# Forget-gate attention: projections by head half, heads placed between k steps, one PSUM bank per head

## The reference

```python
def forgetting_mixer(h, w_in, b_f, w_out):
    proj = h @ w_in                                   # 1024 -> 3 * 1024 + 16
    qkv = proj[..., :3 * ATTN_WIDTH].reshape(B, S, 3, N_HEADS, HEAD_DIM)   # 16 heads of 64
    q, k, v = qkv[:, :, 0], qkv[:, :, 1], qkv[:, :, 2]
    log_f = log_sigmoid(proj[..., 3 * ATTN_WIDTH:] + b_f)
    c = cumsum(log_f, axis=1)
    # per head:  s = q k^T / 8 + c_i - c_j, causal;  p = softmax(s);  o = p v
    return o @ w_out
```

## Time and profile before

| what | value |
|---|---|
| time, median of 3 runs | 2292.36 us (2290.62 to 2293.33) |
| span of the profiled execution, first to last instruction | 2288.1 us |
| PE busy | 2171.5 us, 95% of the span |
| DVE busy / ACT busy | 1228.2 us (54%) / 1006.8 us (44%) |
| mean granted TensorE clock | 0.940 of full |
| the fox stage, first q0 matmul to first FFN matmul | 1950.58 to 2089.11 us |

### The profile page before, as it was taken

One profiled execution on the slowest core, in us unless ns is written; L12 is line 12 of the kernel. 1 busy time (PEld: TensorE's weight loads), 2 busy tenths in 40 slices (PEclk: granted clock), 3 DMA queues, 4 the chain that ended last, 5 costly groups with the idle time before them and its releaser, 6 DMA issues.

```text
span 2288.1 us, 27158 instructions
## 1 busy us (share of the span) xinstructions
PE 2171.5 (95%) x9922; PEld 1783.3 (78%) x9930; DVE 1228.2 (54%) x1280; ACT 1006.8 (44%) x1233; POOL 262.7 (11%) x387
## 2 busy tenths in 40 slices
PE   7999979899999999889999899999999999999997
PEld 5887857788878878677788787778777887887886
DVE  4555589755555556698654544235325545545554
ACT  5445744544444446645444344224314444454442
POOL 1000195000000000680000023002100000000000
PEclk9999989999999999989999999579758999999999
DMA  6554433445545554325455545015203554424552
GB/s 233 197 183 176 167 142 123 165 174 189 195 150 202 190 196 166 138 98 185 164 184 189 186 147 184 1 60 185 87 0 127 186 190 177 147 93 147 184 183 100
DMA packets 53476, 354.22 MB, mean 155 GB/s; under 512 B 7440, under 2 KB 8080, under 8 KB 11536
## 3 DMA queue, kind: packets, MB, share of 16 engines
q1 hardware_dynamic: 53392, 353.10, 43.2%
HBM read 352.03 MB, written 1.05 MB: 154 GB/s over the span
## 4 chain that ended last, share of the span: by engine, by line
PE 82%; DVE 8%; ACT 3%; issue 2%; DVEq 2%; POOL 1%; POOLq 1%; ACTq 0%; DMA 0%; SPq 0%
PE psum L1460 55%; PE psum L1516 15%; PE psum L1606 4%; PE psum L1635 3%; DVE wlo L849 3%; DVE arena L1023 2%; PE psum L1616 2%; DVEq L1017 1%; ACT whi L478 1%; PE psum L1526 1%; PE psum L1558 1%; PE psum L1604 1%; PE psum L1472 1%; DVE arena L1034 0%; ACT arena L608 0%
## 5 line engine op out<-in xcount | busy, mean ns | idle before, releaser
L849 DVE TENSOR_TENSOR wlo<-raw,whi 128x2048 fp32r<-128x2048 f32 x325 | 745.6, 2296 | 531.4 <-ACT whi L478 531.4
L1460 PE MATMUL psum<-whi,xTh 128*128 128x512 f32 (+1 forms) x1968 | 781.4, 397 | 32.5 <-DVE xTl L856 17.1
L1460 PE MATMUL psum<-whi,xTl 128*128 128x512 f32 (+1 forms) x1968 | 768.1, 390 | 0.0
L1460 PE MATMUL psum<-wlo,xTh 128*128 128x512 f32 (+1 forms) x1968 | 767.0, 390 | 0.0
L478 ACT ACTIVATE whi<-raw 128x2048 fp32r<-128x2048 f32 x325 | 620.8, 1916 | 280.9 <-PE psum L1516 151.0
L1460 PEld LDWEIGHTS psum<-whi,xTh 128*128 128x128 f32 x1968 | 375.0, 191 | 111.2 <-DVE xTl L856 17.2
L1460 PEld LDWEIGHTS psum<-whi,xTl 128*128 128x128 f32 x1968 | 374.2, 190 | 78.4
L1460 PEld LDWEIGHTS psum<-wlo,xTh 128*128 128x128 f32 x1968 | 375.3, 191 | 72.8
L1516 PE MATMUL psum<-whi,braT 128*128 128x512 f32 x1056 | 337.4, 390 | 6.6 <-DVE braT L967 6.6
L1516 PEld LDWEIGHTS psum<-whi,braT 128*128 128x128 f32 x1056 | 198.2, 188 | 48.9 <-issue 5.4
L1516 PE MATMUL psum<-wlo,braT 128*128 128x512 f32 x528 | 205.5, 389 | 0.0
(11 more groups left out here) (187 smaller groups left out, 1572.0 us busy)
## 6 DMA issues: line engine op xcount, KB each, us to landing
raw<-w_stream SPq DMA_DIRECT2D x327, 1024.0 KB, 4.8
bias<-chunks SPq DMA_DIRECT2D x18, 256.0 KB, 5.0
x<-x_in SPq DMA_DIRECT2D x1, 1024.0 KB, 5.0
arena<-gate_w SPq DMA_DIRECT2D x2, 512.0 KB, 4.8
arena<-fins SPq DMA_DIRECT2D x2, 512.0 KB, 5.6
out<-x SPq DMA_DIRECT2D x1, 1024.0 KB, 4.0
con<-consts SPq DMA_DIRECT2D x1, 784.0 KB, 11.9
vec<-vecs SPq DMA_DIRECT2D x2, 94.5 KB, 4.0
```

Source lines behind the costliest of these rows:

```text
L849: TT(wlo[:, r], raw[:, r], whi[:, r].bitcast(F32), ALU.subtract).then_inc(lo_done, 1)
L1460: ins = pe.matmul(dst(rb), s(kt)[:, rows], w[:, r, at_:at_ + cols], start=start and n == 0 and k == 0, stop=stop and n == len(kts) - 1 and ...
```

## The change

Only the fox stage changes; the arithmetic is the same.

1. The order of units becomes f, q0, k0, v0, q1, k1, v1, and the weight stream is laid out to match. `sums` moves from behind q0 to behind the first k step of q0.
2. `whole` and `attention` are no longer called here. PE gets an order of single k steps (`step`), with the pieces of the heads between them: `scores_of`, `turn_p`, `pv`, and the turns of single row groups (`heads_turn`). Heads 0 to 7 lie between the k steps of q1, k1 and v1.
3. Heads 8 to 15 lie between the k steps of the output projection. Its k steps alternate between the two column halves (`out(0, kt)`, `out(1, kt)`), in an order in which each needs only output tiles that are there; the output's split tiles lie in `braT` and `latT`, and there are six turns of them instead of four (`FOX_O_TILES`).
4. A head has one PSUM bank (4 + h%2) for scores, turned probabilities and output in succession; scores of head h wait until DVE has taken the output of head h-2 out (`fox_out`).
5. DVE takes over the copy of the turned probabilities from ACT (`turned_out`) and scales each head's output by itself (`o_out`, 16 times a reciprocal, a drain and one operation).
6. At the end of the stage the norm's transposes stand between the last k step of column half 0 and that of half 1.

```diff
-FOX_TURNS = (NORM_TURNS + [(f"{qk}{n}", "act" if n % 2 == 0 else "dve") for qk in "qk" for n in range(8)]
-             + [(f"o{n}", "split") for n in range(4)])
+FOX_TURNS = (NORM_TURNS + [(f"{qk}{n}", "act" if n % 2 == 0 else "dve") for half in range(2) for qk in "qk" for n in range(4 * half, 4 * half + 4)]
+             + [("o1", "split")] + [(f"o{n}", "split") for n in range(2, 6)])
+FOX_TURNS.insert([n for n, _ in FOX_TURNS].index("k4"), ("o0", "split"))
+FOX_O_TILES = [(0, 1), (2, 3), (4,), (5,), (6,), (7,)]
...
 ACT, new order from the splits on
+                split(b, 7)
+                exp(0)
+                exp(1)
+                split(b, 8)
+                rows("q", 1)
+                split(b, 9)
+                exp(2)
...
+                exp(14)
+                exp(15)
+                o_hi(4)
+                o_hi(5)
+                split(b, 16)
                 next_norm(b)
...
 DVE
+                def turned_out(h):
+                    dve.wait_ge(p_turned, fox_place(b, h))
+                    if h >= 2:
+                        dve.wait_ge(pv_done, fox_place(b, h - 2))
+                    dve.tensor_copy(x_pt[h % 2], psum[:, 4 + h % 2, 0:3 * P]).then_inc(pt_dve, 1)
+                def o_out(h):
+                    dve.wait_ge(exp_done, fox_place(b, h))
+                    dve.reciprocal(rden[:, 2 * h:2 * h + 2], den[:, 2 * h:2 * h + 2])
+                    dve.drain()
+                    dve.wait_ge(pv_done, fox_place(b, h))
+                    TT(x_o[:, :, h * HD:(h + 1) * HD], psum[:, 4 + h % 2, 0:2 * HD]...).then_inc(fox_out, 1)
...
+                upto(6)
+                v_out(0)
+                upto(7)
+                largest(0)
+                largest(1)
+                upto(8)
+                turned_out(0)
+                o_out(0)
+                turned_out(1)
+                upto(9)
+                largest(2)
+                o_out(1)
...
+                residual(units.place("wo0"), 1.0, ready, ((0, 0), (0, 1)))
+                next_norm(b)
+                residual(units.place("wo0"), 1.0, ready, ((1, 0), (1, 1)))
+                upto(16)
...
 PE
-                todo = [None, turns("q", x_q, 0), turns("q", x_q, 1), turns("k", x_k, 0), turns("k", x_k, 1), first_scores]
-                for n, name in enumerate(("q0", "q1", "k0", "k1", "v0", "v1")):
-                    whole(b, units, name, 1 + 2 * n, 2, W, xh, xl, never, between=todo[n])
-                    if n == 0:
-                        sums()
-                turns_left(b, plan, "k7")
-                run(first=2)
-                pe.wait_ge(o_done, o_count[0])
-                row_turns(b, plan, ("o0", "o1"), x_o)
-                out_proj(b, plan, units, "o", 13, lambda: row_turns(b, plan, ("o2", "o3"), x_o[:, :, W:]))
+                step("q0", 1, 0)
+                sums()
+                for kt in range(1, 8):
+                    step("q0", 1, kt)
+                for kt in range(8):
+                    step("k0", 3, kt)
+                    if kt >= 4:
+                        heads_turn("q", kt - 4)
+                for kt in range(8):
+                    step("v0", 5, kt)
+                    if kt % 2:
+                        heads_turn("k", kt // 2)
+                step("q1", 7, 0)
+                scores_of(0)
+                step("q1", 7, 1)
+                step("q1", 7, 2)
+                scores_of(1)
+                step("q1", 7, 3)
+                step("q1", 7, 4)
+                turn_p(0)
+                step("q1", 7, 5)
+                step("q1", 7, 6)
+                pv(0)
+                turn_p(1)
+                step("q1", 7, 7)
...
+                out(0, 5)
+                scores_of(14)
+                pv(13)
+                out(1, 5)
+                turn_p(14)
+                scores_of(15)
+                o_turns(4)
+                pv(14)
+                out(0, 6)
+                turn_p(15)
+                out(1, 6)
+                pv(15)
+                o_turns(5)
+                out(0, 7)
+                norm_turns(b.next)
+                out(1, 7)
```

More of the change, by code:

```diff
@@ L806, in fox @@
[L806 to L828, removed]
+                split(b, 1)
+                split(b, 2)
+                rows("q", 0)
+                act.wait_ge(fox_pe, 1)
+                c = psum[:, 4, 0:RB * NH].rearrange("p (r h) -> p r h", r=RB)
+                act.activation(x_q[:, :, :, HD + 1], c, ACT.Copy)
@@ new lines, in fox @@
+                split(b, 9)
+                exp(2)
+                tiles_out("q", 4)
+                exp(3)
+                split(b, 10)
+                tiles_out("q", 6)
+                exp(4)
+                exp(5)
+                rows("k", 1)
+                split(b, 11)
+                o_hi(0)
+                tiles_out("k", 4)
+                exp(6)
+                split(b, 12)
+                exp(7)
+                tiles_out("k", 6)
+                split(b, 13)
+                exp(8)
@@ L1277, in v_out, with largest @@
                     ins.then_inc(udve, 1)
-                upto(10)
-                v_out(0)
-                upto(12)
[L1282 to L1285, removed]
+                def largest(h):
+                    dve.wait_ge(s_in, fox_place(b, h))
+                    for rb in range(RB):
+                        ins = dve.reduce_max(negmax[:, 2 * h + rb:2 * h + rb + 1], psum[:, 4 + h % 2, rb * P:rb * P + (rb + 1) * P], AX, negate=True)
+                    ins.then_inc(max_done, 2)
@@ new lines, in fox @@
+                turned_out(3)
+                largest(4)
+                o_out(3)
+                turned_out(4)
+                largest(5)
+                tiles_out("q", 7)
+                upto(11)
+                o_out(4)
+                turned_out(5)
+                o_lo(0)
+                largest(6)
+                o_out(5)
+                tiles_out("k", 5)
+                upto(12)
+                turned_out(6)
+                largest(7)
+                o_out(6)
+                turned_out(7)
@@ new lines, in fox @@
+                tiles_out("k", 7)
+                o_out(7)
+                v_out(1)
+                largest(8)
+                upto(13)
+                o_lo(1)
+                largest(9)
+                turned_out(8)
+                o_out(8)
+                turned_out(9)
+                largest(10)
+                o_out(9)
+                turned_out(10)
+                largest(11)
+                o_out(10)
+                turned_out(11)
+                upto(14)
+                o_lo(2)
@@ new lines, in fox, with ready @@
+                largest(12)
+                o_out(11)
+                turned_out(12)
+                largest(13)
+                upto(15)
+                o_lo(3)
+                o_out(12)
+                turned_out(13)
+                largest(14)
+                o_out(13)
+                turned_out(14)
+                largest(15)
+                o_lo(4)
+                o_out(14)
+                turned_out(15)
+                o_out(15)
+                o_lo(5)
+                def ready(c, rb):
+                    dve.wait_ge(slot_used, b.slot + 16 + c)
@@ new lines, in scores_of @@
+                def scores_of(h):
+                    if h % 2 == 0:
+                        if h // 2 % 2:
+                            pe.wait_ge(tdve, b.tdve + plan.upto(f"k{h // 2}", "dve", "split"))
+                        else:
+                            pe.wait_ge(tact, b.tact + plan.upto(f"k{h // 2}", "act"))
+                    if h >= 2:
+                        pe.wait_ge(fox_out, h - 1)
+                    for rb in range(RB):
+                        keys = (rb + 1) * P
+                        dst = psum[:, 4 + h % 2, rb * P:rb * P + keys]
+                        pe.matmul(dst, identb[:], maskb[:, P - rb * P:2 * P], start=True, stop=False)
+                        ins = pe.matmul(dst, x_qT[0:HD + 2, h, rb * P:(rb + 1) * P], x_kT[0:HD + 2, h, 0:keys], start=False, stop=True)
+                    ins.then_inc(s_in, 2)
@@ new lines, in o_turns, with step @@
+                def o_turns(n):
+                    tiles = FOX_O_TILES[n]
+                    pe.wait_ge(fox_out, 2 * (tiles[-1] + 1))
+                    turn(b, plan, f"o{n}", [(k * S + rb * P, x_o[:, rb, t * P:(t + 1) * P]) for k, t in enumerate(tiles) for rb in range(RB)])
+                def step(name, i, kt):
+                    if kt == 0:
+                        unit_free(b, units, name)
+                    u = units.place(name)
+                    ins = use(b, i + kt // 4, [(kt, kt % 4 * W)], W, xh, xl, never, lambda rb: pair(u)[:, rb], kt == 0, kt == 7)
+                    if kt % 4 == 3:
+                        ins.then_inc(slot_used, 1)
@@ new lines, in out @@
+                def out(c, kt):
+                    if kt in (0, 2, 4, 5, 6, 7):
+                        name = "o%d" % [t[0] for t in FOX_O_TILES].index(kt)
```

(60 more changed lines are left out.)

159 lines of the change are left out of this document (122 added, 37 removed).

## The result

The changed kernel takes 2306.42 us (median of 4 runs, 2306.14 to 2310.05), the kernel before, in the same session, 2291.77: a ratio of 1.0064, 95% interval 1.005 to 1.0079. That is 14.65 us more; forecast were 2309 and 16.7 more. The spans of the two profiled executions differ by more (2308.1 against 2288.1), because the profiled one of the changed kernel is the slowest of its four and had lost 4.5 us before it reached the changed stage. So the parts are compared from the stage's own start.

A forecast was written before the change was run, and what follows sets the result against it. The prediction took PE, busy 95% of the span, to bound the kernel. Sums +9.3, k0 to the FFN +3.4 (119.7 work plus 9.15 waits against 125.5) and clock +4.0 gave 16.7 on 2292.4: 2309 us, range 2297 to 2322.

The forecast's parts named there:

- The sums: In q0, PE idles 7.6 us at the moved sums for DVE's logarithm, then runs at half clock: +9.3 us.
- the upper bound: Upper bound of the sums' term: half clock for 6.6 us behind the wait, +10.4 us.
- PE's own work from k0 on: From k0 to the FFN, PE's work without waits takes 119.7 us, 5.8 below the present 125.5.
- The waits: From k0 to the first FFN step, PE waits 9.15 us in all; bounds no wait to twice the waits.
- the walk through the orders: PE, DVE and ACT orders followed side by side from k0's start with assumed prices, giving 9.15 us of PE waits.
- The clock in the interleaved part: Half clock behind a little over two of three waits, some 1.8 us each: +4.0 us, bounds 0 and 9.
- The sum: All terms of the change together: 9.3 + 3.4 + 4.0 = 16.7 us more, median 2309.
- Rival 1: Heads hide cleanly: attention waits stay as small as before, clock full; +4.5 us, 2297; chance 0.10.
- Rival 2: Faster: heads' small matmuls cost PE much less between long ones; -8.5 us, 2284, at 1.1 us a head; chance 0.04.
- rival 3: Waits compound: heads land behind the next split, 11 splits each cost PE about 2 us; +29.5, 2322; chance 0.10.
- rival 4: Clock never settles: frequent waits from q1 on keep PE's mean clock at 0.75; +35 us, 2327; chance 0.05.

The follow-up runs named there:

- e1: The changed kernel with the sums back behind all 8 k steps of q0: 2296.01 us, ratio 1.0009 to the kernel before.
- e2: The kernel before with only the sums moved, behind the first k step of q0: 2302.84 us, ratio 1.0036 to the kernel before.
- e4: e1 with, on DVE, the copy of head 0's turned probabilities ahead of the split of slot 10: 2292.85 us, ratio 1.0002.
- e6b: e4 with, on ACT, the high part of output tile 6 ahead of head 15's exponentials: 2290.69 us, ratio 0.9993.
- e5b: e4 with output projection k steps one place later and, on ACT, exp(11) ahead of the split of slot 16: 2290.11 us, ratio 0.9991.
- e7b: e5b with k step out(1,6) behind out(0,7) instead of ahead of it: 2289.47 us, ratio 0.9988.
- e8: e7b with, on DVE, head 2's maxima and heads 1 and 2's outputs ahead of splits (slots 11, 12): 2288.72 us, ratio 0.9986.
- e3: The changed kernel with the sums behind the fourth k step of q0 instead of the first: 2304.37 us, ratio 1.0043.

## Why the prediction was right

- **The sums.** Forecast +9.3, measured +10.3; e1 and e2 show the cause from both sides. PE stood as long as forecast: the sums began 10.25 us behind q0's first matmul, where 10.3 had been reckoned. What followed was taken too small. The half clock lasted 5.7 us where 4.1 had been put in (the upper bound had 6.6), which is 0.8 us, and the three sums took 1.30 us for 1.0. One sentence of the prediction is wrong: that PE restarts at the half clock after such a wait. Here and in e2 the clock was low before the wait began. In the stretch that it read the rule from, the matmuls at 665.92, 666.26 and 666.50, behind 3.9 us of idle time, stand at full-clock distances, and the steps of 0.43 us begin only at 667.07:

```profile
665.92 0.50 PE L1460 MATMUL psum<-whi,xTh 128*128 128x512 f32 x1 [3.92 <-DVE xTl L856]
666.26 0.39 PE L1460 MATMUL psum<-wlo,xTh 128*128 128x512 f32 x1
...
667.07 0.63 PE L1460 MATMUL psum<-wlo,xTh 128*128 128x512 f32 x1
```

The Trainium skill, in TensorE: Matmul & The Clock Gate, section What's actually happening, says that the throttled clock is the default and that activity lifts it. The traces agree: q0 starts at a granted clock of 0.50 behind the gate's product of 16 columns and reaches the full clock amid its 512 column matmuls, in the kernel before after about 3.1 us.
- **PE's own work from k0 on.** Forecast 119.7. Where the clock stayed full all the way it can be read off. In e4's window from k0 to the FFN PE is busy for 118.97 us:

```profile
1966.34:2091.62 125.28, 118.97 (x667) 97.83 (x666) 66.23 (x118) 53.35 (x108) 0.00 (x0) 1.00 0.33 118
```

- **The waits.** Forecast 9.15 in ten places, measured 7.15 (130.07 less the 122.92 busy), of which 7.01 in seven places. The 0.85 for the turn of head 2 and the small ones for tile 4 and the first FFN step did not show in this execution. Each of the others stood where the walk through the orders had put it: `pv(0)` 1.73 for 1.6, tile 5 0.69 for 0.8, tile 6 1.56 for 1.8, head 15 0.38 for 0.65, tile 7 0.93 for 1.2, the norm 1.38 for 1.65, and scores 4 0.34 for 0.25. In the tail each forecast was 0.1 to 0.3 too long; which price of the walk made it so was not looked into. The new operations cost about what was assumed: the copy 0.55 us (0.5), the output 0.29 (0.25). e4 and e6b each show the cause of one wait (`pv(0)`, tile 6); e5b and e7b show that a k step of cover takes away those for tiles 5, 6 and 7 and that at the norm.
- **The clock in the interleaved part.** Forecast +4.0, measured 3.9 (122.92 busy less 119.0). The prediction took a little over two falls in three places. Two came: behind `pv(0)` (2019.09 to 2022.49) and behind tile 7 up to the norm turns (2100.69 to 2108.05); behind tile 6 none came. The size was right, the mechanism only in part, and that the number fits this execution so well is luck: a wait of 1.4 to 1.7 us is sometimes followed by the half clock and sometimes not, in the same place of nearly the same kernel (e1, e4, after). Which wait brings it down is not settled by these runs.
- **The sum.** The terms' misses partly cancel: the sums were 1.0 too low, the waits 2.0 too high, PE's own work 0.7 too high, the clock 0.1. So the total, 16.7 for 14.9 in the stage, is off by less than the waits alone.
- **Rivals.** Rival 1, clean hiding, is right for the middle window, where PE idled for 2.2 us, and wrong for the serial tail, which was not hidden. Rival 2, faster, is out: with heads at 1.3 us each in place of 1.85 PE's own work would have been 8.8 us below 119.7, and it was 118.97. The waits did not compound (rival 3), and the clock was 0.96 over the second part, not 0.75 (rival 4).

Where the expected gain of the interleaving went: with no wait and the full clock it could win 125.5 - 119.0 = 6.5 us. The changed kernel lost 7.15 in waits and 3.9 in clock against that, which leaves it 4.6 slower there, and the sums took 10.3 on top. With the orders of e4, e5b, e7b and e8 together, 4.5 of the 6.5 are there (125.52 to 121.02, in e8).

## What to carry to other kernels

Before an instruction with a wait is moved ahead on a bound engine, look up when the awaited result is there, counted from a fixed point: the row of the logarithm's last step told the 7 us beforehand. Look also at the clock there: a wait moved to where the clock has just risen, or is about to, costs the slow start once more. When small dependent pieces are laid between long work, the in-order queues of the *helpers* decide: put what the bound engine waits for ahead of 2 us of bulk work there, and keep some bulk steps of the bound engine for the end, where the chain is serial. Measure first how much idle time there is to win.

## What the hardware showed unexpectedly

The price of a fall did not follow the length of the wait. Behind 7.34 us, with the clock low beforehand, the half clock lasted 5.7 us (after) and 6.1 (e2); behind 3.08 us, with the clock full beforehand, 6.6 (e3).

Nor did the fall follow the length among the short waits. Waits of 1.72 us (e1), 1.73 (e3, at `pv(0)`) and 1.56 (e4) left the clock at full, waits of 1.73 (after) and 1.55 us (e1 and e3, tile 6) did not, and in the changed kernel and in e3 it fell behind the 0.93 us for tile 7, while in e4 the same wait (0.94) left it full. The fall could come late: at `pv(0)` the half clock began 1.5 us after PE had gone on.

Since this differs between executions, two kernels of this kind should be compared by their waits and by busy time in windows at full clock, or by many runs.
